# A two-layer transformer block on one core: the feed-forward in two passes over the tokens, with the norm of the first pass's tiles inside the second

## The reference, cut to what matters

```python
def post_norm(h, y, gate, g, b):
    return layer_norm(DN_ALPHA * h + gate * y, g, b)

def swiglu_sublayer(h, shift, scale, gate, w_g, w_u, w_d, g, b):
    u = modulate(h, shift, scale)
    f = (jax.nn.silu(u @ w_g) * (u @ w_u)) @ w_d
    return post_norm(h, f, gate, g, b)
```

## Time and profile before

| | us |
|---|---|
| median of 3 runs (lowest, highest) | 4265.39 (4264.25, 4266.76) |
| the profiled execution | 4264.5 |
| its span, first to last instruction | 4262.2 |

### The profile page before, as it was taken

The page is one execution under the profiler, slowest core; times in us unless marked ns, Lnnn a source line. Parts: engine busy times, 40 slices in busy tenths (PEclk is TensorE's granted clock), DMA queues, the critical chain, the costliest instruction groups (busy, mean ns, idle before and its releaser), DMA issues. The chain is left out here.

```text
span 4262.2 us, 52025 instructions
## 1 busy us (share of the span) xinstructions
PE 3553.8 (83%) x19550; PEld 2828.6 (66%) x19550; DVE 1611.0 (38%) x2555; ACT 1299.4 (30%) x2242; POOL 1434.5 (34%) x951
## 2 busy tenths in 40 slices
PE   6799596878686999999995599596966969999991
PEld 2488386555475888888881387385654758888881
DVE  2104553756472221121126404555845621222215
ACT  2211274765442011101103311375844321111111
POOL 1211242763344223323322311244923433333331
PEclk8899697788898999999997799698988979999996
DMA  8423312113331111111105323312033311111112
GB/s 287 151 86 116 100 26 64 30 37 84 102 105 58 40 40 39 34 34 44 39 15 202 132 90 111 95 31 71 15 88 90 99 59 50 49 49 49 43 36 93
DMA packets 151200, 318.19 MB, mean 75 GB/s; under 512 B 12105, under 2 KB 72489, under 8 KB 151057
## 3 DMA queue, kind: packets, MB, share of 16 engines
q1 hardware_dynamic: 128304, 260.20, 19.6%
q10 hardware_dynamic: 19072, 44.60, 2.8%
q0 software_dynamic: 3680, 11.47, 1.0%
HBM read 250.20 MB, written 66.03 MB: 74 GB/s over the span
## 5 line engine op out<-in xcount | busy, mean ns | idle before, releaser
L2061 POOL TENSOR_TENSOR ffn_wlo<-ffn_raw,ffn_whi 128x1024 fp32r<-128x1024 f32 x132 | 314.6, 2390 | 800.3 <-ACT ffn_whi L2032 800.3
L2125 DVE TENSOR_TENSOR ffn_hid<-ffn_up,ffn_silu 128x512 f32<-128x512 f32 (+1 forms) x110 | 70.2, 638 | 1049.0 <-PE ffn_up L127 1022.9
L2032 ACT CAST ffn_whi<-ffn_raw 128x1024 fp32r<-128x1024 f32 x132 | 136.4, 1048 | 945.1 <-PE ffn_acc L127 467.4
L2130 DVE TENSOR_TENSOR y<-ffn_acc,y 128x512 f32<-128x512 f32 x396 | 273.8, 691 | 266.8 <-PE ffn_acc L127 266.8
L125 PE MATMUL ffn_gate<-second_uhi,ffn_whi 128*128 128x512 f32 (+1 forms) x880 | 325.9, 370 | 37.3 <-POOL ffn_wlo L2061 37.3
L126 PE MATMUL ffn_gate<-second_ulo,ffn_whi 128*128 128x512 f32 (+1 forms) x880 | 325.3, 370 | 0.0
L127 PE MATMUL ffn_gate<-second_uhi,ffn_wlo 128*128 128x512 f32 (+1 forms) x880 | 325.1, 369 | 0.0
L126 PE MATMUL ffn_up<-second_ulo,ffn_whi 128*128 128x512 f32 (+1 forms) x880 | 323.9, 368 | 0.0
L125 PE MATMUL ffn_up<-second_uhi,ffn_whi 128*128 128x512 f32 (+1 forms) x880 | 323.8, 368 | 0.0
L127 PE MATMUL ffn_up<-second_uhi,ffn_wlo 128*128 128x512 f32 (+1 forms) x880 | 323.7, 368 | 0.0
L125 PE MATMUL ffn_acc<-ffn_whi,ffn_hhi 128*128 128x512 f32 x792 | 308.2, 389 | 0.0
(11 more groups left out here) (270 smaller groups left out, 8157.8 us busy)
## 6 DMA issues: line engine op xcount, KB each, us to landing
ffn_raw<-w_ffn_dram SPq DMA_DIRECT2D x132, 512.0 KB, 3.6
in_raw<-w_in_dram SPq DMA_DIRECT2D x42, 512.0 KB, 3.5
norm_input_ada_w<-w_ada_dram SPq DMA_DIRECT2D x10, 2048.0 KB, 9.2
norm_ffn_ada_w<-w_ada_dram SPq DMA_DIRECT2D x8, 2048.0 KB, 8.0
proj_scratch<-in_stage ACTq DMA_DIRECT2D x20, 640.0 KB, 2.9
ada_w<-w_ada_dram SPq DMA_DIRECT2D x6, 2048.0 KB
gla_kq<-proj_scratch SPq DMA_DIRECT2D x32, 320.0 KB
swa_qhl<-heads_scratch SPq DMA_DIRECT2D x36, 256.0 KB
```

The lines of the kernel that those rows point to most:

```text
L2032: act.copy(whi[:, j % 3, :], raw[:, j % 3, :]).then_inc(w_hi, 1)
L2061: pool.tensor_tensor(wlo[:, j % 3, :], raw[:, j % 3, :], whi[:, j % 3, :].bitcast(F32), ALU.subtract).then_inc(w_ready, 1)
L2125: dve.tensor_tensor(hf[:, c, 0:tn], UP[:, c, 0:tn], sg[:, c, 0:tn], ALU.mult).then_inc(mul_done, 1)
L2130: dve.tensor_tensor(Y[:, tt, cols], ACC[:, half, :], Y[:, tt, cols], ALU.add).then_inc(y_added, 1)
```

## The change

Feed-forward (`swiglu`, now with its norm):

- The tokens go in two passes over all 11 groups. Layer 0: 768 tokens (chunks of 512 and 256: tiles 2 to 5, 0 and 1), then the last 512; layer 1: 512, then 512. Every weight tile is loaded and split in each pass. A pass with one chunk takes f = 0 with 512 columns and f = 1 as two parts of 256.
- `raw` has 2 buffers in place of 3, silu, gate and up two each, used in turn by all parts. The product of silu and up stays in the silu's buffer (`hf` is gone), and silu waits for the split of the part before last. The first group copies into `y`, so it isn't zeroed.
- Under the second pass the tiles of the first are normed, one in each of the groups 1, 2, 4, 5, 7, 8 (layer 0, six tiles) or 1, 2, 4, 5 (layer 1, four tiles). The last four tiles are normed behind the last group, in the same program, with residuals loaded into `raw`, `whi` and `wlo`.
- The loop over groups is written out.
- The program `norm_tiles("ffn")` is gone, and with it its modulation chunks: the eight chunks (4 to 11 of layer 1) are now made in the windowed attention of layer 1 (`modulation_chunk`), one in each of the tiles 2 to 5 and two in 6 and 7, as 32 matmuls with a stationary of 32 columns, four weight buffers, a row addition on DVE, stores from ACT.

```diff
-        chunked = modulated and not attn
+        chunked = kind == "input"
...
+            chunks = [(1, c) for c in range(4, ADA_CHUNKS)]
+            shares = [0, 0, 1, 1, 1, 1, 2, 2]
...
+            def modulation_chunk(b, n):
+                pe.wait_ge(w_in[n % AR], 80 * (n // AR + 1))
+                pe.wait_ge(c_set, 3)
+                if b >= 2:
+                    pe.wait_ge(o_done, b - 1)
+                k = n - chunks_at(b)[0]
+                if k:
+                    pe.wait_ge(row_done, n)
+                for kt in range(KT):
+                    for j in range(4):
+                        mm = pe.matmul(O[32 * j:32 * j + 32, b % 2, k * P:(k + 1) * P], cs[:, kt, :], W[:, n % AR, kt, j * P:(j + 1) * P],
+                                       start=(kt == 0), stop=(kt == KT - 1))
+                mm.then_inc(product_done, 1)
...
+        def alone(chunk):
+            t0, tn = chunk
+            return [[(t0, tn)], [(t0, tn // 2), (t0 + tn // 2, tn // 2)]]
+        passes = [alone(CHUNKS[0]) if last else [[CHUNKS[0], CHUNKS[2]]] * 2, alone(CHUNKS[1])]
+        WIDTH = sum(tn for _, tn in passes[0][1])
+        normed_tiles = sorted(tt for t0, tn in passes[0][1] for tt in range(t0 // P, (t0 + tn) // P))
+        NT = len(normed_tiles)
+        left_tiles = [tt for t0, tn in passes[1][1] for tt in range(t0 // P, (t0 + tn) // P)]
+        NL = len(left_tiles)
+        all_tiles = normed_tiles + left_tiles
+        group_of = [1 + 3 * k // 2 for k in range(NT)]
+        raw = sb(nm + "raw", [P, 2, D])
...
+            def load_weight(p, g, j):
+                w = weight(p, g, j)
+                if w >= 2:
+                    sp.wait_ge(w_ready, w - 1)
+                sp.dma_start(raw[:, w % 2, :], t["w_ffn"][layer][(g * 6 + j) * P:(g * 6 + j + 1) * P, :]).then_inc(raw_in[w % 2], 16)
...
+            for p in range(2):
+                for g in range(G):
+                    if p == 0 and g == 1:
+                        load_residual(0)
+                    for j in range(6):
+                        load_weight(p, g, j)
+                        if j == 3 and p == 1 and g - 1 in group_of:
+                            k = group_of.index(g - 1)
+                            store(k)
+                            if k + 1 < NT:
+                                load_residual(k + 1)
...
+            def silu(p, g, f):
+                for c, (t0, tn) in enumerate(passes[p][f]):
+                    n = unit(p, g, f, c)
...
+            for p in range(2):
+                for g in range(G):
+                    k = norm_tile(p, g)
+                    if k is not None:
+                        normalize(k, 0, Y[:, all_tiles[k], :])
+                    silu(p, g, 0)
+                    split(p, g, 3)
+                    split(p, g, 4)
+                    silu(p, g, 1)
+                    split(p, g, 5)
+                    if k is not None and not last:
+                        if k == 0:
+                            act.wait_ge(one_plus, 1)
+                        normalize(k, 1, x[:, :])
+                        modulate(k)
+                    if following(p, g)[0] < 2:
+                        for j in range(3):
+                            split(*following(p, g), j)
+
+            def high_part(k):
...
+            for p in range(2):
+                for g in range(G):
+                    k = norm_tile(p, g)
+                    split(p, g, 3)
+                    if not last and norm_tile(p, g - 1) is not None:
+                        low_part(norm_tile(p, g - 1))
+                    if k is not None:
+                        scaled(k)
+                    hidden(p, g, 0)
+                    split(p, g, 4)
+                    split(p, g, 5)
+                    hidden(p, g, 1)
+                    if following(p, g)[0] < 2:
+                        for j in range(3):
+                            split(*following(p, g), j)
...
+                    for n, (c, tt, at) in enumerate(tiles_of(p)):
+                        pe.wait_ge(hid_ready, unit(p, g, 1, c) + 1)
+                        if n == 2 and norm_tile(p, g) is not None and not last:
+                            turn(norm_tile(p, g))
...
+            for p in range(2):
+                for g in range(G):
+                    k = norm_tile(p, g)
+                    if not last and norm_tile(p, g - 1) is not None:
+                        high_part(norm_tile(p, g - 1))
+                    if k is not None:
+                        residual(k)
+                        normalizers(k, 0)
+                    multiply(p, g, 0)
+                    if k is not None:
+                        shifted(k)
+                        if not last:
+                            normalizers(k, 1)
+                    multiply(p, g, 1)
+                    if (p, g) != (1, G - 1):
+                        for n in range(len(tiles_of(p))):
+                            accumulate(p, g, n)
+
...
                 norm_tiles(nc, t, res, "attention", layer, tiles, False)
                 with ExitStack() as inner:
                     res["y"] = inner.enter_context(nc.sbuf_tensor(f"y{layer}", [P, TILES, D], F32))
-                    swiglu(nc, t, res, layer, LAT_CHUNKS if last else CHUNKS)
-                    norm_tiles(nc, t, res, "ffn", layer, tiles, last)
+                    swiglu(nc, t, res, layer, last)
                 if not last:
                     input_projection(nc, t, res, layer + 1)
```

452 lines of the change are left out of this document (328 added, 124 removed).

## The result

| | median, us | ratio to the kernel before, 95% interval |
|---|---|---|
| before | 4264.8 | |
| changed | 4238.1 | 0.9946, 0.9933 to 0.9958 |
| changed, six further runs on another chip | 4237.4 | 0.9947, 0.9934 to 0.9960 |

What follows compares the result with a forecast made beforehand. TensorE bounds the feed-forward stages; the 262 us after their last matmuls, where DVE, ACT, POOL and stores pass tiles, can be won. 16 + 69 - 106 - 57 - 7 + 32 = -53 gives 4212 us, range 4160 to 4250.

Steps and rivals of the forecast that it cites:

- part 1, passes: Feed-forward in two passes: matmul time +6.6 us in layer 0, +13.1 in layer 1, loop turns -3; sum +16.
- part 2, tiles under pass 1: Six and four tiles normed under the second pass: stalls 43.5 us in layer 0, 15.4 in layer 1, clock 10; sum +69.
- part 3, tails: After the last feed-forward matmul only four tiles are left: -106 us in layer 0, -57 in layer 1.
- zeroing of y: POOL's zeroing of y (8.63 us) goes in both layers, about half of it in the way: -7 us.
- part 4, chunks and memsets: Eight modulation chunks moved to layer 1's windowed attention +30 us, rows and stores +1, memsets in both layers +1: +32.
- the walk: Queues followed through tile groups, first (1, 4, 7) and second (2, 5, 8) of a pair, and tails; 4185 to 4240, chance 0.69.
- a restart costs some 2 us at half clock in five groups: 10: In tile groups, stalls of 6 to 10 us lower TensorE's clock; restarts in five groups add 10 us.
- the 0.18 us a turn: Feed-forward loop's cost per turn, taken from 82.32 against 82.14 us a group; 18 turns gone give -3 us.
- Tables at double cost: Rival: every ACT table switch costs double in the norm groups and tails, +29 us: 4241; chance 0.07.
- The slow chain of POOL: Rival: with two raw buffers POOL's chain sets every single-part group, up to +112 us: 4324; chance 0.09.
- The hidden norm: Rival: norm under the second pass fully hidden, residual in time, stalls near 0: 4143, partly 4165; chance 0.15.
- The chunks' waits: Rival: each chunk in windowed attention holds TensorE 3 us through its DVE row, +24: 4236; inside the range, no chance given.

Runs made afterwards that it cites:

- run 9: Changed kernel with new work orders on ACT, POOL and DVE, the residual asked for early, and a third raw weight buffer: ratio 0.9771 to the kernel before.
- Run 6: Changed kernel with the residual asked for early and 12 idle TensorE products in each tile group's stop before the down products: ratio 0.9833 to the kernel before.
- run 5: Changed kernel with nothing normed under the second pass, those tiles stored as plain sums one group later: ratio 0.9697 to the kernel before.
- run 12: Changed kernel with the modulation chunks cut to one of eight products deep, their loads, rows and stores kept: ratio 0.9914 to the kernel before.
- run 3: Changed kernel with a third raw weight buffer: ratio 0.9892 to the kernel before.
- run 10: Changed kernel with early residual, new queue orders, and the first norm of second-pass tiles done by DVE alone in two passes: ratio 0.9738 to the kernel before.
- runs 8: Changed kernel with new work orders on ACT, POOL and DVE and the residual asked for early: ratio 0.9814 to the kernel before.

## Why the prediction was right or wrong

The sum against the two profiled executions:

| term | forecast | measured | from |
|---|---|---|---|
| part 1, passes | +16 | +25 | layer 0: 52.06 + 10 x 49.97 + 11 x 33.30 = 918.1 for 907.4; layer 1: 368.9 + 366.3 for 721.0 |
| part 2, tiles under pass 1 | +69 | +98 | the ten rows |
| part 3, tails | -163 | -159 | layer 0: 80.81 - 10.9 = 69.9 for 173.1; layer 1: 43.86 - 10.9 = 33.0 for 88.7 |
| zeroing of y | -7 | -6 | 3.4 and 2.6, from the norm's last transpose to the first gate product |
| part 4, chunks and memsets | +32 | +21 | windowed attention with its ends: +18.3 in layer 1, +2.5 in layer 0 |
| not of the change | 0 | -5 | 4.6 of it ahead of the first changed instruction |
| sum | -53 | -26 | |

The miss in the terms is larger than the 27 us of the sum. Parts 1 to 3 and the zeroing cost 43 us more than forecast; part 4 cost 11 less, and 5 us are not of the change. That these two hide a part of the miss is luck.

**Part 2 failed, in two of its numbers.** First, the walk took each duration from a row in which the other engine was out of the way. "DVE: last addition 0.7, gate, residual, statistics 4.1: 4.8" is 6.9, since the residual pass waits for POOL's subtraction (+2.1); with POOL's late low part (+0.9) that makes the 3 us by which the first groups are longer apart from the clock: stop and transposes 5.5 instead of 2.5 in layer 0, 2.8 instead of 0.1 in layer 1. That these two waits make the 3 us is read from the trace; no run takes them away alone, and run 9 shows that they cost 0.3 us a group in layer 1 under other orders. For the second groups the walk was near: 11.5 against 12, 8.1 and 8.8 against 7.6. All stops and transposes together: 73.5 for 58.9. Second, the clock: "a restart costs some 2 us at half clock in five groups: 10". The price was right (1.6 to 1.9), the count was not: nine of ten groups pay, the second ones twice, 24.4. The prediction expected the low clock only behind stops of 6 to 10 us; here stops of 2.3 to 3.3 us were followed by it too. Run 6 shows the term by itself, run 5 that nothing else hides in these groups.

**Part 3** held within 4 us, but not tile by tile: on DVE the tiles of layer 1 follow each other every 8.8 us instead of 7.0, since the residual pass takes 3.28 us again, and the 3 us of waiting in the walk cover half of these three waits; in layer 0 they follow every 12 to 14 us. **Part 1** was 9 short: a first-pass group of layer 0 takes 49.97 us instead of 49.5, which is 5 us in eleven, and the 33 groups of 33.30 are each 0.1 over the 33.2 taken, 3 us. So groups written out also stand over the count of their products, and the 0.18 us a turn that the prediction gave to the loop, worth 3 us to it, need not be the loop's. **Part 4** was 11 too dear: a record with 32 stationary columns costs 0.027 us by run 12, half of the 0.058 taken as "nearer to the same operation". The products were 16 us too dear, and some 5 us of memsets, rows and loads had been left out. Why these records are faster than the prologue's 0.045 (four column strips in turn here, two columns alone there) was not tried.

**The rivals.** Tables at double cost: wrong; ACT's load at 1973.61 is followed by silu at 1974.90. That rule of the Trainium skill ("ScalarE: Activation LUTs", "What ACT_TABLE_LOAD costs") is not borne out here: no drain shows. The sums with it, 4241 and 4242, are close to the result for another reason, by luck. The slow chain of POOL: wrong, plain groups take 33.3 with two buffers as with three (run 3). The hidden norm: not in this order of queues, but reachable; run 10 has it in layer 1. The chunks' waits: some 2.5 us in that stage by proportion, not 24.

Of the signs named ahead, "36 us in the first and 45 in the second group of a pair" came out as 40 and 48, the tails as 70 and 33 for 67 and 31, windowed attention of layer 1 as 18 us longer for 30. The signs that would have spoken against the mechanism (plain groups over 34 us, gaps at table loads, pairs of equal length) did not show: the mechanism was right, and two terms of part 2 were too small, the stops of the first groups and the clock.

## What to carry to other kernels

Work that is to be hidden under a full engine has a price on every queue that it shares: give each added wait a place behind what the full engine needs next, and ask for its data a group ahead (orders and early residual alone gave 56 us). Count a stop of TensorE of about 3 us at nearly 5 unless a trace says otherwise, and count how many there are, not only how long. Where DVE and POOL both pass over SBUF at a place that TensorE waits for, add up their times. What helped most here was to let DVE do both steps of the norm (33 us between runs 8 and 10, with two roots side by side on ACT in the same edit).
